# Products of an opening and of two mixing stages put into other places of TensorE's program, with part of VectorE's and GpSimd's work handed over

## What is computed

```python
# block 1 (x, c)
sh1, sc1, gt1, sh2, sc2, gt2 = split(silu(c) @ w_mod + b_mod)      # w_mod: 1024 x 6144
a = rms_norm(x, g_norm_mix) * (1 + sc1) + sh1
f = fft2(a in 4 groups of 256 channels, axes=(tokens, channels), norm="ortho").real
x = x + gt1 * (f @ w_fnet_out)
x = x + gt2 * conv_ffn(rms_norm(x, g_norm_ffn) * (1 + sc2) + sh2)   # 1024 -> 2 x 2816 -> 1024
x = rms_norm(x, g_final)
# block 2
x = x + 0.5 * swiglu(rms_norm(x))                                   # 1024 -> 2 x 2816 -> 1024
p = rms_norm(x) @ w_in                  # columns: r, k, v (512 each), w, a, g (low rank), pool (512)
p_rw = p_rw + (token_shift(p_rw) - p_rw) * mu
# 8 heads of 64: state = state * w_t + (state @ -kk_t) (kk_t a_t)^T + v_t k_t^T ; y_t = state @ r_t
y_rw = (group_norm(y) * ln_w + ln_b + bonus) * g
y_pool = (sliding means of 2, 4, 8, 16 tokens minus p_pool) @ w_pool * pool_scale
x = x + concat(y_rw, y_pool) @ w_out
x = x + 0.5 * swiglu(rms_norm(x))
out = rms_norm(x)
```

## Time and profile before

| what | value |
|---|---|
| median of 3 runs | 1459.3 us (1458.4 to 1459.77) |
| the profiled execution, its own time | 1457.89 us |
| its span, first to last instruction | 1456.1 us |
| TensorE busy (matmul) | 1422.5 us, 98% |
| TensorE weight loads | 1171.5 us, 80% |
| VectorE / ScalarE / GpSimd busy | 530.8 / 508.5 / 788.0 us |
| mean granted TensorE clock | 0.998 of full |
| HBM read | 154.04 MB |

### The profile page before, as it was taken

How to read it: one execution, slowest core, us unless ns; L and a number is a source line. 1 busy time by engine, 2 the same in 40 slices (tenths; PEclk the granted TensorE clock), 3 DMA queues, 4 the chain that set the end, 5 groups by cost and what they waited for, 6 DMA issues and landing times.

```text
span 1456.1 us, 21745 instructions
## 1 busy us (share of the span) xinstructions
PE 1422.5 (98%) x8088; PEld 1171.5 (80%) x8088; DVE 530.8 (36%) x716; ACT 508.5 (35%) x719; POOL 788.0 (54%) x1034
## 2 busy tenths in 40 slices
PE   7999999999999999999999999999999999999997
PEld 5887888888888788888888877877788888888887
DVE  6976422222002842222200268885453222221003
ACT  6424433333122523323211367425443332332222
POOL 1763745545555864554555577663466455455543
PEclk9999999999999999999999999999999999999999
DMA  9872432222322232232233222200133323323221
GB/s 365 342 299 94 140 116 100 101 101 86 102 101 87 82 106 101 86 103 98 90 103 96 87 89 71 75 16 3 57 105 101 101 86 101 101 86 103 99 72 58
DMA packets 45705, 156.96 MB, mean 108 GB/s; under 512 B 5328, under 2 KB 8656, under 8 KB 45520
## 3 DMA queue, kind: packets, MB, share of 16 engines
q1 hardware_dynamic: 45648, 156.16, 31.1%
HBM read 154.04 MB, written 2.10 MB: 107 GB/s over the span
## 4 chain that ended last, share of the span: by engine, by line
PE 85%; DVE 7%; issue 3%; ACT 3%; POOL 1%; DMA 0%; DVEq 0%; SPq 0%; POOLq 0%; ACTq 0%
PE ps L1768 27%; PE ps L1770 26%; PE ps L1769 26%; POOL w_lo L544 1%; DVE tri_p L1215 1%; DVE tri_x L1215 1%; PE ps L2234 1%; DVE mid_sq L1218 1%; DVE act_lo L1218 1%; ACT w_hi L740 1%; DVE rAR L1218 0%; PE ps L1788 0%; DVE pads L1215 0%; PE ps L2290 0%; DVE rB L1215 0%
## 5 line engine op out<-in xcount | busy, mean ns | idle before, releaser
L544 POOL TENSOR_TENSOR w_lo<-raw,w_hi 128x256 fp32r<-128x256 f32 x932 | 694.0, 778 | 566.1 <-ACT w_hi L740 565.7
L1768 PE MATMUL ps<-act_hi,w_hi 128*128 128x512 f32 x1328 | 522.5, 393 | 5.2 <-DVE act_lo L1218 2.0
L1770 PE MATMUL ps<-act_hi,w_lo 128*128 128x512 f32 x1328 | 517.0, 389 | 0.0
L1769 PE MATMUL ps<-act_lo,w_hi 128*128 128x512 f32 x1328 | 516.8, 389 | 0.0
L740 ACT ACTIVATE w_hi<-raw 128x1024 fp32r<-128x1024 f32 x233 | 244.8, 1054 | 431.0 <-PE ps L1770 404.1
L1768 PEld LDWEIGHTS ps<-act_hi,w_hi 128*128 128x128 f32 x1328 | 249.3, 188 | 63.6 <-issue 4.5
L1769 PEld LDWEIGHTS ps<-act_lo,w_hi 128*128 128x128 f32 x1328 | 249.4, 188 | 52.1 <-issue 1.4
L1770 PEld LDWEIGHTS ps<-act_hi,w_lo 128*128 128x128 f32 x1328 | 249.3, 188 | 52.1
L1768 PE MATMUL ps<-hid_hi,w_hi 128*128 (+2 forms) x588 | 219.9, 374 | 0.8 <-issue 0.8
L1769 PE MATMUL ps<-hid_lo,w_hi 128*128 (+2 forms) x588 | 219.7, 374 | 0.0
L1770 PE MATMUL ps<-hid_hi,w_lo 128*128 (+2 forms) x588 | 219.7, 374 | 0.0
(11 more groups left out here) (281 smaller groups left out, 991.8 us busy)
## 6 DMA issues: line engine op xcount, KB each, us to landing
raw<-weight_units SPq DMA_DIRECT2D x233, 512.0 KB, 3.5
wm_mid<-mod_units SPq DMA_DIRECT2D x18, 512.0 KB, 7.5
wm_ring<-mod_units SPq DMA_DIRECT2D x14, 512.0 KB, 8.5
wm_early<-mod_units SPq DMA_DIRECT2D x8, 512.0 KB, 7.7
wm_late<-mod_units SPq DMA_DIRECT2D x8, 512.0 KB, 6.8
x_tok<-tokens SPq DMA_DIRECT2D x4, 512.0 KB, 6.2
xT<-tokens_by_channel SPq DMA_DIRECT2D x1, 2048.0 KB, 8.3
result<-act_out SPq DMA_DIRECT2D x16, 128.0 KB, 1.8
```

Source lines behind the costliest of these rows:

```text
L544: ins = nc.gpsimd.tensor_tensor(w_lo[:, slot, c], raw[:, slot, c], w_hi[:, slot, c].bitcast(f32), SUB)
L1768: nc.tensor.matmul(o, wh, xh, start=start, stop=False, **check)
L1769: nc.tensor.matmul(o, wh, xl, start=False, stop=False, **check)
L1770: return nc.tensor.matmul(o, wl, xh, start=False, stop=stop, **check)
```

## The change

**Opening.** The high part of x's first token tile is made in two halves, with the table's high part between them. TensorE no longer waits for the low parts of tile 0: `first_block` makes all seven high x high products first, then the seven with x's low part, then the seven with the table's. Two units of the shift, i = 14 and 15, are taken as columns (`last_columns`: 16 products of 128 x 128 and the eight column sums of the shift), and stand ahead of the channel transforms t = 6 and 7 instead of behind t = 7. VectorE sums one unit less; of its early sums (before SC1 is read) there is one less. SyncE's transfer of `xT` and the loads into the slots of i = 14 and 15 wait for the shift's columns.

**Input projection.** Gate products, key scaling and grams move from between units into later units (`inner_products`). The banks of the pool units are read by ScalarE (`pool_out`), which only copies; GpSimd multiplies with `rstd` later (four operations). VectorE's order changes: `raw_removal(1)` and `(3)` stand ahead of the `shifted` of their step, `removal(0)` one step earlier, and `removal(3)` behind `normed`. On ScalarE `tri_out` stands ahead of `high_n` at step 9. The last two bonus products follow unit 15 instead of 16.

**Pairs.** Pair 0 makes K first. One `keep_busy` product stands in every front between AV and G1. In the second and fifth stage on TensorE one f moves between MT/N and S1/RO. The last two triangle blocks of pair 0 are copied by VectorE. `pool_hi(3)` moves one place ahead, and the gate of the last pair goes from GpSimd to VectorE.

```diff
-BY_COLUMN = 2 * KT - 1
+BY_COLUMN = 2 * KT - 2
 def sums_through(i):
-    return i + (i < BY_COLUMN)
+    return min(i + 1, BY_COLUMN) if i < 2 * KT else i + 1 - (2 * KT - BY_COLUMN)
...
                 if i == 3 * KT - 1:
-                    sp.wait_ge(sem("wm_used"), sums_through(2 * KT - 3))
+                    sp.wait_ge(sem("mod_mm"), mod_turn(SH1))
                     sp.dma_start(xT[:, :, :], a_xt).then_inc(sem("loaded_once"), 16)
...
             second_factor(0)
             second_factor(1)
+            for g in range(len(WINDOWS)):
+                pool.wait_ge(sem("pool_read"), g + 1)
+                n_chain[0] += 1
+                nc.gpsimd.tensor_tensor(pooled[:, g, :], pooled[:, g, :], rstd[:, :], MUL).then_inc(sem("pool_chain"), 1)
+                pool.wait_ge(sem("pool_chain"), n_chain[0])
...
             out_low("RO")
-            gated(3)
             out_low("Y")
...
-                nc.scalar.activation(xn_hi[:, t * D:(t + 1) * D], x_tok[:, t, :], ACT.Copy).then_inc(sem("in_hi"), 1)
+                first = D // 2 if t == 0 else D
+                nc.scalar.activation(xn_hi[:, t * D:t * D + first], x_tok[:, t, 0:first], ACT.Copy).then_inc(sem("in_hi"), 1)
                 after(sem(f"loaded_cs{t}"), 32)
                 after(sem("x_rstd"), t + 1)
                 nc.scalar.activation(cs_hi[:, t * NY:(t + 1) * NY], cs_raw[:, t, :], ACT.Copy, scale=x_ss[:, t:t + 1]).then_inc(sem("in_hi"), 1)
+                if t == 0:
+                    nc.scalar.activation(xn_hi[:, first:D], x_tok[:, 0, first:D], ACT.Copy).then_inc(sem("in_hi"), 1)
...
+            def pool_out(g):
+                i = IN_ORDER.index(("pool", g))
+                after(unit_used, U_IN + i + 1)
+                nc.scalar.activation(pooled[:, g, :], ps[:, i % 4, :], ACT.Copy).then_inc(sem("pool_read"), 1)
...
                 pool_hi(1)
                 pool_hi(2)
-                yield
                 pool_hi(3)
+                yield
                 act.wait_ge(tensor_step[1], at(PE_STEPS, PAIRS - 1, "Y"))
...
-            for i in range(2, KT + 3):
+            for i in range(2, KT + 2):
                 wm(i)
             mod_out(SC1)
...
-            for i in range(KT + 3, BY_COLUMN):
+            for i in range(KT + 2, BY_COLUMN):
                 wm(i)
...
                 if i == 8:
-                    for q in range(PAIRS):
-                        removal(q)
-                if name == "pool":
-                    pool_input(p)
-                else:
+                    removal(1)
+                    removal(2)
+                if name != "pool":
                     normed(name, p)
+                    if i == 5:
+                        raw_removal(1)
+                    if i == 6:
+                        raw_removal(3)
+                    if i == 7:
+                        removal(0)
+                    if i == 8:
+                        removal(3)
                     if i >= 9:
                         solve_steps(1)
                     shifted(name, p, {"wa": wa[:, 0, :], "gx": gx[:, 0, :], "k": pk[p], "r": rt[:, p % 2, :], "v": rV[:, p, :]}[name])
...
+            def last_gate(p):
+                after(scalar_step[p % 2], at(AC_STEPS, p, "bias"))
+                for n, (o, x, op) in enumerate(((rB, rBonus, ADD), (rG, rG, MUL))):
+                    after(vector_step[p % 2], at(VE_STEPS, p, "yn") + n)
+                    nc.vector.tensor_tensor(o[:, p, :], rB[:, p, :], x[:, p, :], op).then_inc(vector_step[p % 2], 1)
...
-            for k in range(TT_):
+            def first_block(x, cs, start):
+                for m in range(KT - 1):
+                    if start and m == KT // 2:
+                        after(sem("in_hi"), 3)
+                    nc.tensor.matmul(ps[:, seq_bank(m), :], x[:, m * P:(m + 1) * P], cs[:, 0:NY], start=start, stop=False)
+
+            after(sem("in_hi"), 2)
+            first_block(xn_hi, cs_hi, True)
+            after(sem("x_lo"), 1)
+            first_block(xn_lo, cs_hi, False)
+            after(sem("cs_lo"), 1)
+            first_block(xn_hi, cs_lo, False)
+            for k in range(1, TT_):
...
+            def last_columns():
+                for i in range(BY_COLUMN, 2 * KT):
+                    after(wm_full[wm_place[i][1]], 16 * wm_place[i][2])
+                for m in range(KT):
+                    o = LAST_COLUMN + m
+                    for i in range(BY_COLUMN, 2 * KT):
+                        k = i - KT
+                        nc.tensor.matmul(ps[:, 7, o:o + P], wm_buf(wm_place[i][0])[:, m * P:(m + 1) * P], c_silu[:, k:k + 1].to_broadcast([P, P]), start=i == BY_COLUMN, stop=i == 2 * KT - 1)
+                mod_columns(SH1)
+
             after(lo_done, U_DFT + 1)
             for t in range(KT):
+                if t == KT - 2:
+                    last_columns()
...
-            n, flag, turn, _ = wm_place[BY_COLUMN]
-            after(wm_full[flag], 16 * turn)
-            for m in range(KT):
-                nc.tensor.matmul(ps[:, 7, LAST_COLUMN + m:LAST_COLUMN + m + P], wm_buf(n)[:, m * P:(m + 1) * P], c_silu[:, KT - 1:KT].to_broadcast([P, P]), start=True, stop=True)
-            mod_columns(SH1)
             after(sem("f_new"), 3)
             keep_busy(DC_BANK, 3)
             after(sem("y_lo"), KT + 1)
...
-                if i == 4:
-                    gate_product(0)
-                    gate_product(1)
                 if i == 5:
-                    gate_product(2)
-                    gate_product(3)
                     key_sums(0)
                 if i == 6:
                     key_sums(1)
-                if i == 7:
-                    for p in range(PAIRS):
-                        key_scale(p)
-                if i == 8:
-                    for p in range(PAIRS):
-                        triangle_grams(p)
...
+            def inner_products(i, k):
+
+                if i == 5 and k == 1:
+                    gate_product(0)
+                    gate_product(1)
+                if i == 6 and k == 1:
+                    gate_product(2)
+                    gate_product(3)
+                if i == 8 and k == 3:
+                    for p in range(PAIRS):
+                        key_scale(p)
+                if i == 9 and k == 3:
+                    triangle_grams(0)
+                    triangle_grams(1)
+                if i == 9 and k == 6:
+                    triangle_grams(2)
+                    triangle_grams(3)
...
+                for part in (keys, values, removals) if p == 0 else (values, removals, keys):
+                    part()
+                    yield
...
                 ve_did("LR")
+                keep_busy(b.bank, 1)
                 ac_did("AVa")
                 ve_did("AVb")
...
-            in_stages(front, back, closing, ("ffffffffnfnf", "fbbbfbfbfbfbfbfbfb", "ffbfbbfbfbfbfbfbfbfb", "ffbfbbfbfbfbfbfbfbfb", "bbfbfbfbfbfbfbffbffffb"))
+            in_stages(front, back, closing, ("ffffffffnfnf", "bfbbfbfbfbfbfbfbfb", "ffbfbbfbfbfbfbfbfbfb", "ffbfbbfbfbfbfbfbfbfb", "bfbbfbfbfbfbfbffbffffb"))
```

More of the change, by code:

```diff
@@ L196, in at @@
 def at(steps, pair, name):
-    return pair // 2 * len(steps) + steps.index(name) + 1
+    order = PE_FIRST if steps is PE_STEPS and pair == 0 else steps
+    return pair // 2 * len(steps) + order.index(name) + 1
 def pool_at(pair, name):
@@ L462, in load_wm @@
                 n, flag, _, before = wm_place[i]
-                if before == BY_COLUMN:
+                if before is not None and BY_COLUMN <= before < 2 * KT:
                     sp.wait_ge(sem("mod_mm"), mod_turn(SH1))
@@ L1626, in front @@
                         over_chunks(masks[:, g, :], NCP), MUL))
+                if p == 0:
+                    after(sem("cleared"), cleared_through("TT0"))
+                    for e in (2, 3):
+                        triangle_block(nc.vector.tensor_copy, p, e)
                 yield
@@ L1855, in unit_by_output @@
                         owed()
+                    if within is not None:
+                        within(k)
                 last.then_inc(unit_used, 1)
@@ L2211, in front, with values @@
-                did("K", last)
-                yield
+                def values():
+                    if p >= 2:
+                        pe.wait_ge(vector_step[p % 2], at(VE_STEPS, p - 2, "y"))
+                        pe.wait_ge(scalar_step[p % 2], at(AC_STEPS, p - 2, "sq"))
+                    elif p == 1:
+                        after(sem("prep"), 2)
+                    else:
+                        bank_read(IN_ORDER.index(("pool", 2)))
+                    after(sem("centre"), 2)
+                    for c in range(NCP):
+                        cols = slice(c * P, (c + 1) * P)
+                        last = nc.tensor.matmul(bank(0)[:, cols], rV[:, p, cols], cent, start=True, stop=True)
+                    did("tV", last)
@@ new lines, in removals @@
+                def removals():
+                    if p == 0:
```

(25 more changed lines are left out.)

88 lines of the change are left out of this document (30 added, 58 removed).

## The result

The changed kernel takes 1460.8 us (median of 22 executions, 1459.5 to 1462.7), the kernel before 1458.4 (22 executions, 1457.2 to 1461.9): a ratio of 1.0015 with a 95% interval of 1.0009 to 1.0021. It is 2.4 us slower; I had forecast 2.0 us faster. Within 0.2% it counts as no change, but the interval leaves 1.0 out, so the sign of the forecast was wrong. The profiled execution took 1460.56 us with a span of 1458.5, against 1457.89 and 1456.1 before.

A forecast was written before the change was run, and what follows sets the result against it. TensorE's matmuls, 98% of the span, were taken as the bound. Opening +1.0, input projection -1.9 and pairs -1.1 summed to -2.0 us: 1457.3 us on medians (1455.9 against the profiled execution), 80% range 1453.0 to 1460.8.

The forecast's parts named there:

- Opening, start: First product at 7.85 us instead of 9.79, 1.9 us earlier; 1.1 if the clock rises at the same moment as now.
- 4.4 us after the first product: Opening: TensorE's clock rises from 1.2 to 2.4 GHz this long after its first product, keeping the whole 1.9 us.
- Opening, sums: Opening: eight more column products cost 1.8 us and a wait for VectorE's last sum 1.0; first output unit 1.0 us later overall.
- rival 4: Whole kernel: if waits made TensorE's clock fall, fillers would give something back; held to cost tenths; no chance given.
- key sums: Input projection, behind unit 5: sums of squared keys come 3.1 us earlier, giving a new TensorE wait of 1.1 us.
- Input projection: Removed waits -4.4, new costs +0.15, +1.1, +0.5 and +0.7: -1.9 us in sum, bounds -4 and +1.8.
- (c): Input projection: raw_removal(1) ahead of k3's shifted makes key norms 1.7 us later; key scaling waits about 0.5 us, between 0 and 4.
- rival 2: Input projection: moved products find everything ready, so it gives -3.5 instead of -1.9; 1455.7 us, 20%.
- Rival 3: Input projection: key chain becomes the bound, key norms 5.5 us late, TensorE stands in unit 8: +3.7, 1461.0 us, 12%.
- Pair 0: Pair 0's front: K first, VectorE has four pool inputs less and ends before TensorE needs it; the filler fits the wait.
- Fillers: Pairs' fronts: one 0.65 us product each, fitting pair 0's wait, +0.1 in each other; +0.4 with pair 0, between 0 and 1.
- Fifth stage: Pool product fills the wait ahead of S1, pool_hi(3) removes a 1.30 us wait: together -1.65 us, between -0.8 and -2.2.

The follow-up runs named there:

- opening_alone: The kernel before with only the change's opening edits (first block by parts, two shift sums as columns, shift's columns ahead of the sixth transform): 1461.7 us, ratio 1.0027.
- clock_held: The changed kernel plus three filling products, one ahead of the wait for SC1's last sum, two ahead of the second key tile's squares: 1459.1 us, ratio 1.0004.
- opening_held: opening_alone plus one filling product of 384 columns ahead of the wait for the last sum of SC1: 1461.9 us, ratio 1.0020 to the kernel before.
- input_alone: The kernel before with only the input projection's edits, pair 0's waits adapted to the two counters: 1456.3 us, ratio 0.9983.
- blocks_by_scalar: The changed kernel with pair 0's two triangle block copies back on ScalarE: 1459.4 us, ratio 1.0006 to the kernel before.
- closing_alone: The kernel before with only the fifth stage's edits (last gate on VectorE, pooled products a place later, high parts in new order): 1458.0 us, ratio 0.9997.
- columns_alone: The kernel before with only the opening's columns (sixteen column products, shift's columns ahead of the sixth and seventh transforms), first block as before: 1462.2 us, ratio 1.0026.

## Why the prediction was wrong

**Opening, start: right in kind, too large.** 7.58 us for the first product against 7.85 forecast (the terms given add up to 7.82). Of the 1.9 us expected, the first transform shows 0.9 in the changed kernel; the six profiles of kernels with the late start have it at 36.75 on average, the five with the early start and no fall at 35.3: 1.4 us. One term that was off is the clock's rise "4.4 us after the first product": in the 13 profiles without products on the vectors' tile it comes 3.0 to 6.2 us after it. The other is that the read of SC1 was taken to move with VectorE's sum: in opening_alone it waits 0.64 us for TensorE's column sums, in clock_held 1.05. In opening_held, where the clock rose after 3.0 us, that read doesn't wait and the transforms start at 34.47, about as forecast. The Trainium skill (TensorE: Matmul & The Clock Gate, What's actually happening) says just that the moment of the rise differs from run to run, and these profiles agree; I named it and took the better end.

**Opening, sums: right.** Forecast +1.8 for the eight products and +1.0 for the wait; measured +2.6 to +2.7 together, in five kernels without a fall there. With the start at -1.4 the opening is +1.3 without falls by these stretches, against +1.0. The times say more, as below.

**The clock: the first step that failed.** I dismissed rival 4 with "with waits up to 1.3 us the mean granted clock is 0.998". One execution's clock was all that I had, and at least 24 of 121 of the same kernel have a fall. The change adds waits beside narrow products (1.1 us forecast at the key sums, 1.0 measured), and I priced them at their length. In the profiled execution the two falls explain 1.6 us in the opening (58.4 instead of the 56.7 forecast) and about 1.3 in the input projection. In the medians the clock is worth less: clock_held, with the falls gone, gives back 1.7 of the 4.4 us between forecast and result, and that is the figure that an experiment shows. The other 2.7 us, but for what the three products cost themselves, come from elsewhere. Why a fall comes in every execution of the changed kernel, and in only 3 and 4 of 11 of opening_alone and input_alone, is open.

**Input projection: the sum was right by luck.** Forecast -1.9, in the changed kernel -1.6, but from other terms: (c), the late key norms, cost nothing: the key scaling did not wait. Without a fall the stage gives -2.6 (input_alone) to -2.9 (clock_held), between my sum and rival 2's -3.5. Rival 3 did not come.

**Pair 0: a term at zero that was 1.4.** "VectorE now has four pool inputs less and ends before TensorE needs it" looked at the queue's length, not at its last items. The diff puts two block copies, 2.3 us, ahead of the masking that G1 waits for, on the one engine where they are on the path; blocks_by_scalar gives 1.4 us back. K first itself cost nothing: in blocks_by_scalar pair 0's front stands 0.2 behind, a filler's share.

**Fillers: 0.8 (medians, hardly clear of noise) to 1.0 (profiles) instead of 0.4.** I had put them at +0.1 each behind pair 0, as if most of a product of 0.65 us fitted into the waits; by the profiles it is 0.7 for the three.

**Fifth stage: right by the profiles.** -1.65 forecast, -1.6 in the changed kernel; the median of closing_alone shows 0.4.

So, in the profiled execution: opening +1.7 off by the clock, input projection +0.3, pair 0 +1.4, fillers and the swap in stages 2 to 4 +0.9. In medians: 1.7 by the clock, 1.4 by the block copies, 0.4 by the fillers, if these add; that is 3.5 of 4.4 us. What stays open is the opening: its medians (+3.2, +3.5, +3.8 in opening_alone, opening_held and columns_alone) are 1.1 to 2.2 us more than stretch by stretch explains with 1.3, 1.3 and 2.7. Falls don't explain it, since in executions at 0.998 alone the means are still +2.7, +2.4 and +4.1. In their profiles 1.8 us of opening_alone's and 0.9 of columns_alone's come behind G1, where the code is that of before; why, no run shows.

## What to carry to other kernels

In this kernel a wait added on TensorE among narrow products cost its length and, in some or all executions, half clock behind it; look at the granted clock by stretch, and over many executions, before calling a wait harmless. The mean clock of an execution counts the end of the kernel too, so small differences in it are no sign of a fall. When work changes hands between engines, look at what the receiving engine has queued behind it at that moment, not at how idle it is on average. And when two engines reach a point within some tenths of a microsecond of each other, as TensorE and VectorE's w_mod sums do here, making one faster gives no more than those tenths.

## What the hardware showed

The clock fell behind 0.6 and 1.0 us of idle time with sixteen narrow products beside it (29.4 to 32 and 882.4 to 885 us); where both waits were filled with wide products, the profile shows it up and none of 11 executions has a mean under 0.997. The Trainium skill (TensorE: Matmul & The Clock Gate, HAM oscillation — how this bites in real kernels) tells of falls behind long idle gaps; these gaps were short. The filler at the opening's wait didn't do the same in opening_held, where 3 of 12 executions still fell. And the same instructions gave mean clocks of 0.993 to 0.998 and times of 1456.3 to 1463.7 us over 121 executions of the kernel before, so that a single profile without a fall doesn't show that a kernel has none.
